# Feature sums by matmul: a moving operand of 1, 2 or 16 columns widened to 128 columns

## The reference

```python
def rmsnorm(x, g):                       # before every mixer and every MLP, and at the end
    var = jnp.mean(x * x, axis=-1, keepdims=True)
    return x * lax.rsqrt(var + EPS) * g

def l2norm(x):                           # over the 128 features of a head
    return x * lax.rsqrt(jnp.sum(x * x, axis=-1, keepdims=True) + 1e-6)

def gated_deltanet(hn, w_in, conv_w, a_log, dt_bias, out_norm_g, w_out):
    proj = hn @ w_in                                   # q, k, v, z, and 2 x 8 logits a token
    qkv = silu(causal_depthwise_conv_2(proj[..., :3 * DN_DIM], conv_w))
    z = proj[..., 3 * DN_DIM:4 * DN_DIM]
    b_raw, a_raw = proj[..., 4 * DN_DIM:...], proj[..., 4 * DN_DIM + DN_HEADS:]
    q, k = l2norm(heads(q)) * DN_HEAD_DIM ** -0.5, l2norm(heads(k))
    beta = sigmoid(b_raw)
    g = -exp(a_log) * softplus(a_raw + dt_bias)
    o = chunk_gated_delta_rule(q, k, v, g, beta)
    o = rmsnorm_2(o, out_norm_g) * silu(z)             # over the 128 features of a head
    return o.reshape(b, t, DN_DIM) @ w_out

# layer 1: attention and a gated recurrence, silu MLP (2816); layer 2: gated_deltanet, squared-relu MLP (4096);
# layer 3: block attention, squared-relu MLP (4096); then the last rmsnorm
```

## Time and profile before

| | |
|---|---|
| time, median of 3 runs | 1207.03 us (1206.67 to 1207.73) |
| profiled execution, its own time | 1205.23 us |
| its span, first to last instruction | 1203.5 us |
| mean TensorE clock granted in it, 1 being full speed | 0.976 |
| PE busy | 1149.0 us, 95% of the span |
| DVE busy | 752.5 us, 63% |
| ACT busy | 564.8 us, 47% |
| POOL busy | 219.4 us, 18% |
| data moved | 187.34 MB, mean 156 GB/s |

### The profile page before, as it was taken

How to read it: one execution, slowest core, us unless ns; L and a number is a source line. 1 busy time by engine, 2 the same in 40 slices (tenths; PEclk the granted TensorE clock), 3 DMA queues, 4 the chain that set the end, 5 groups by cost and what they waited for, 6 DMA issues and landing times.

```text
span 1203.5 us, 21847 instructions
## 1 busy us (share of the span) xinstructions
PE 1149.0 (95%) x8900; PEld 1111.0 (92%) x8900; DVE 752.5 (63%) x913; ACT 564.8 (47%) x721; POOL 219.4 (18%) x226
## 2 busy tenths in 40 slices
PE   4999899999999999999999999999989999999997
PEld 4999889999999999998999998889989999888996
DVE  3755875666566553579968577764466657776433
ACT  4546456535444343456645355543344445554331
POOL 4894001402000000236372020000030002000001
PEclk9999899999999999889989899999989999999999
DMA  9744443654555555335420155555535545555531
GB/s 268 237 150 141 141 141 106 210 175 150 166 184 190 185 175 174 106 122 185 131 89 2 36 161 189 177 186 192 178 106 177 172 132 183 177 187 190 182 139 36
DMA packets 154852, 187.34 MB, mean 156 GB/s; under 512 B 6400, under 2 KB 143776, under 8 KB 154784
## 3 DMA queue, kind: packets, MB, share of 16 engines
q1 hardware_dynamic: 149072, 183.51, 46.9%
q10 hardware_dynamic: 5712, 2.86, 0.9%
HBM read 185.29 MB, written 1.07 MB: 155 GB/s over the span
## 4 chain that ended last, share of the span: by engine, by line
PE 85%; DVE 9%; issue 2%; ACT 2%; DMA 1%; POOL 1%; SPq 0%; DVEq 0%; POOLq 0%; ACTq 0%
PE PS L332 20%; PE PS L334 19%; PE PS L333 19%; PE PS L383 10%; PE PS L385 5%; DVE WL L328 2%; DVE XHL L480 1%; PE PS L392 1%; PE PS L391 1%; PE PS L390 1%; ACT WH L319 1%; PE PS L1793 1%; PE PS L1779 1%; DMA RAW<-in_w_in 1%; PE PS L672 1%
## 5 line engine op out<-in xcount | busy, mean ns | idle before, releaser
L328 DVE TENSOR_TENSOR WL<-RAW,WH 128x2048 fp32r<-128x2048 f32 x173 | 409.0, 2365 | 252.4 <-ACT WH L319 252.4
L319 ACT ACTIVATE WH<-RAW 128x2048 fp32r<-128x2048 f32 x173 | 330.0, 1910 | 248.4 <-PE PS L334 200.8
L332 PE MATMUL PS<-XHL,WH 128*128 128x256 f32 x1184 | 348.9, 295 | 27.6 <-DVE WL L328 17.2
L333 PE MATMUL PS<-XHL,WH 128*128 128x256 f32 x1184 | 342.8, 290 | 0.0
L334 PE MATMUL PS<-XHL,WL 128*128 128x256 f32 x1184 | 342.7, 289 | 0.0
L332 PEld LDWEIGHTS PS<-XHL,WH 128*128 128x128 f32 x1184 | 235.6, 199 | 33.1 <-DVE WL L328 16.9
L333 PEld LDWEIGHTS PS<-XHL,WH 128*128 128x128 f32 x1184 | 235.7, 199 | 0.3
L334 PEld LDWEIGHTS PS<-XHL,WL 128*128 128x128 f32 x1184 | 235.1, 199 | 0.0
L332 PE MATMUL PS<-HH,WH 128*128 (+1 forms) x688 | 195.0, 283 | 4.3 <-DVE SG L1576 2.8
L333 PE MATMUL PS<-HL,WH 128*128 (+1 forms) x688 | 194.7, 283 | 0.0
L334 PE MATMUL PS<-HH,WL 128*128 (+1 forms) x688 | 194.7, 283 | 0.0
(11 more groups left out here) (287 smaller groups left out, 1537.8 us busy)
## 6 DMA issues: line engine op xcount, KB each, us to landing
RAW<-in_mlp_w_up SPq DMA_DIRECT2D x32, 1024.0 KB, 5.4
RAW<-in_mlp_w_down SPq DMA_DIRECT2D x32, 1024.0 KB, 4.9
RAW<-in_w_in SPq DMA_DIRECT2D x28, 1024.0 KB, 5.1
RAW<-in_w_ffn_in_pairs SPq DMA_DIRECT2D x22, 1024.0 KB, 5.1
RAW<-in_dn_w_in SPq DMA_DIRECT2D x16, 1024.0 KB, 5.7
RAW<-in_mb_w_in SPq DMA_DIRECT2D x12, 1024.0 KB, 5.2
RAW<-in_w_ffn_out SPq DMA_DIRECT2D x11, 1024.0 KB, 5.0
RAW<-in_w_attn_out SPq DMA_DIRECT2D x4, 1024.0 KB, 5.2
```

What stands on the lines that cost most here:

```text
L319: act.activation(WH[:, k], RAW[:, k], ACT.Copy).then_inc(hi_done, 1)
L328: dve.tensor_tensor(WL[:, k], RAW[:, k], WH[:, k].bitcast(F32), ALU.subtract).then_inc(lo_done, 1)
L332: pe.matmul(out, wh, xh, start=start, stop=False, skip_group_check=True)
L333: pe.matmul(out, wh, xl, start=False, stop=False, skip_group_check=True)
```

## The change

Every narrow moving operand is made 128 columns wide. The column of ones is taken as the whole 128x128 tile `ONES`, the pair `W2` is repeated 64 times and the 16 logit columns 8 times by a stride of zero. Each result is then 128 columns wide too; of these only the first, the first two or the first 16 are read. The results are laid over each other in PSUM: call n writes columns n to n + 127, so it overwrites all but the first column of call n - 1, and what is read lies where it lay. In the output norm (L1859) the column of head h and token half c moves from 8c + h to 2h + c, so that columns rise in the order in which they are made, and the transposes behind it read them there. The number of instructions and their order on every engine stay as they were, and nothing else is changed.

```diff
@@ norm_sums
                 for c in range(TT):
                     for j in range(KB):
-                        mm = pe.matmul(PS[:, 4, 2 * c:2 * c + 2], XN[:, j, c * P:(c + 1) * P], W2[:, j],
-                                       start=(j == 0), stop=(j == KB - 1))
+                        mm = pe.matmul(PS[:, 4, 2 * c:2 * c + P].rearrange("p (r e) -> p r e", e=2), XN[:, j, c * P:(c + 1) * P],
+                                       W2[:, j, None, :].to_broadcast([P, P // 2, 2]), start=(j == 0), stop=(j == KB - 1))
             else:
                 pe.wait_ge(s_.sq_added, m + 1 - (m > 2))
                 for c in range(TT):
-                    mm = pe.matmul(PS[:, sums_bank(m), c:c + 1], XN[:, 0, c * P:(c + 1) * P], ONES[:, 0:1], start=True, stop=True)
+                    mm = pe.matmul(PS[:, sums_bank(m), c:c + P], XN[:, 0, c * P:(c + 1) * P], ONES[:], start=True, stop=True)
@@ logits, behind dq step 1
                         for k in range(KB):
-                            mm = pe.matmul(PS[:, 3, 256 + 16 * c:272 + 16 * c], H[:, k, c * P:(c + 1) * P], WBA[:, k],
+                            mm = pe.matmul(PS[:, 3, 256 + 16 * c:384 + 16 * c].rearrange("p (r e) -> p r e", e=16),
+                                           H[:, k, c * P:(c + 1) * P], WBA[:, k, None, :].to_broadcast([P, KB, 16]),
                                            start=(k == 0), stop=(k == KB - 1))
@@ l2 norms, behind dz steps 1 and 2
                         sq = (SQK, XN)[u][:, n % 8, (n // 8) * P:(n // 8) * P + P]
-                        mm = pe.matmul(PS[:, 4 + u, n:n + 1], sq, ONES[:, 0:1], start=True, stop=True)
+                        mm = pe.matmul(PS[:, 4 + u, n:n + P], sq, ONES[:], start=True, stop=True)
@@ output norm
                     for c in range(TT):
-                        mm = pe.matmul(PS[:, 4, 8 * c + h:8 * c + h + 1], OSQ[:, h, c * P:(c + 1) * P], ONES[:, 0:1], start=True, stop=True)
+                        mm = pe.matmul(PS[:, 4, 2 * h + c:2 * h + c + P], OSQ[:, h, c * P:(c + 1) * P], ONES[:], start=True, stop=True)
...
-                        at_, n = e * TOK + c * P, 8 * c + 2 * u + e
+                        at_, n = e * TOK + c * P, 4 * u + 2 * e + c
                         mm = pe.transpose(PS[:, RB[u], at_:at_ + P], RNC[:, n:n + 1].to_broadcast([P, P]), IDENT[:])
```

## The result

| | before | after |
|---|---|---|
| median of 6 runs, us | 1206.85 (1206.33 to 1209.23) | 1201.34 (1199.37 to 1201.99) |
| profiled execution, its span, us | 1205.23, 1203.5 | 1201.34, 1199.6 |
| mean granted clock | 0.976 | 0.99 |

The medians differ by 5.5 us. The ratio is 0.995 with a 95% interval of 0.9937 to 0.9963, that is 4.5 to 7.6 us faster. The forecast was 1199.5 in 1196.9 to 1204.3. The part of that range that the forecast held for itself ended at 1200.5; the rival *some falls stay*, with one of its two places, stood at 1201.0.

A forecast was written before the change was run, and what follows sets the result against it. The chain that ended last was 85% PE and 9% DVE, so PE's time counts where PE is awaited. Gains 1.5 + 1.8 + 3.0 + 1.5 = 7.8, less 0.3, leave 7.5 us: 1199.5 us, range 1196.9 to 1204.3.

The forecast's parts named there:

- some falls stay: Rival, chance 0.20: the gaps at L512 and the end of L1859 still bring falls, 1202.5 us; with one of them 1201.0.
- L512, fall at 300: Narrow passes at 298.97 us, after PE idled 1.41 us: the half-clock stretch behind them goes, 1.5 us won (bounds 0 and 1.5).
- L507: Half step behind this burst, 501.11 to 505.55 us: takes 2.9 us instead of 4.44, so 1.5 us won.
- L1706, the burst: Logits burst from 508.85 us: 3.9 us becomes 3.6 at full clock, so 0.3 us won.
- L1706, step 2 behind it: Half-clock work from 512.74 to 518.75 us: 2.6 us to win, priced at nothing because the chain behind `ba_done` hides it.
- second L1720 and last `dz` step: From 601.32 us: burst 4.16 becomes 3.6 us (0.6 won), the step behind it 2.4 won; 3.0 us, all on the path.
- L1859 and `do`: Wide burst to 677.40 us, transposes and two short PE waits: if the clock holds through these, 1.5 us won.
- wider passes: All 180 widened passes: 0.4 us more PE time, partly counted already in other terms, so 0.3 us remains as cost.
- nothing: Rival, chance 0.08: the falls are not due to narrowness, only 0.4 us is added, 1207.4 us.
- The rival of the overlay: Rival, chance 0.04: in calls with ONES, shifted overlapping writes make passes wait for the one before; 9.6 us lost, 1214.8 us.
- absorbed: Rival, chance 0.08: DVE's chain swallows the 1.8 us of `dq`, or POOL the end of `dz`; 2.5 to 3 remain, 1204.3.

The follow-up runs named there:

- the fillers of 128 and 1 columns: The changed kernel plus extra float32 matmuls into an unused bank in three PE gaps, 128 columns wide in one kernel, 1 in the other; 1198.23 and 1198.39 us.

## Why the prediction was right, step by step

| term of the sum | predicted | trace of after | alone |
|---|---|---|---|
| L512, fall at 300 | 1.5 | 1.49 (3.42 us for 4.91) | 1.5 in the trace, 3.1 timed |
| L507 | 1.5 | 1.50 (6.44 for 7.94) | 1.5 in the trace, 2.1 and 1.4 timed |
| L1706, the burst | 0.3 | 0.3 | 0.3 in the trace |
| L1706, step 2 behind it | 0 | 0 | 0 |
| second L1720 and last `dz` step | 3.0 | 3.05 | 3.05 in the trace, 2.9 timed |
| L1859 and `do` | 1.5 | 0.3 (35.78 us for 36.05) | not run |
| wider passes | -0.3 | about 0 | |
| sum | 7.5 | 6.6 | |

The third column sets the trace of after against that of before.

**The clock.** Right at four places of five. That width is the cause, and not chance between executions, is shown by the count over eleven traces (17 of 20 narrow, 0 of 35 wide) and by the fillers of 128 and 1 columns; the rival "nothing" is refuted.

**The cost of the passes.** 32 wide passes take 3.49 us from their first start to the next matmul, 32 narrow ones took 3.50; my 0.4 us for 180 passes was at most that. The table of the Trainium skill that spoke against the change (TensorE: Matmul & The Clock Gate, Back-to-back issue gap) gives more than twice the gap for 128 columns, but for a single matmul on its own. For a stream, as in this kernel, the same section has the spacing set by weight loads and matmuls together, which I had overlooked. This case agrees with the latter: 0.109 us a pass either way, with PEld busy for the whole burst, narrow (3.50 of 3.50 us) and wide (3.50 of 3.50 us, 495.42 to 498.92). The rival of the overlay is refuted in the same rows: L1721, whose calls shift by a column, takes 3.74 us for 32 passes like L1706, whose passes add into the same columns.

**What hides the gain.** The 2.6 us behind L1706 went into PE's waits, as the working had it, but not at AT, the one wait for which it gave a row: that one stayed at 3.18 us, and 3.17 and 3.19 in the kernels with one part. Most of them went into a new wait of 1.68 us for `WL`, at 532.74 with L1706 alone and at 528.30 in after. The rival "absorbed" is refuted: L507 came 2.19 us earlier (495.42 for 497.61) and the transposes behind AT 3.98 (568.28 for 572.26), so the 1.8 us of L507 and L1706 came through.

**The step that failed** is the last: "I take 1.5: 614.80 to 618.20 was nothing but transposes, and the clock stood at 1.00". The clock did hold through the burst and the transposes, but fell at 676.4, just as `do` began, behind 2.02 us in which PE waited for DOL; that wait had even grown, from 1.54 us, since the transposes ahead of it ended earlier. Only 0.3 us was won from the burst to the next layer's matmul, whose rows are, in after and then in before:

```profile
703.59 0.50 PE L383 MATMUL PS<-XHL,WH 128*128 128x512 f32 x1 [0.52 <-DVE XHL L480]
```

```profile
709.95 0.50 PE L383 MATMUL PS<-XHL,WH 128*128 128x512 f32 x1 [0.52 <-DVE XHL L480]
```

Not even this 0.3 is shown to come from the width: over the five traces with a narrow L1859 this stretch took about 36.0 us three times and about 35.2 twice (the fall was 3.4 us long in these two and 6.8 in the others), and with a wide one and no wide fillers 35.8 in all four. So it is the rival *some falls stay*, with one place of its two. That its 1201.0 lies next to the measured 1201.34 is in part luck: the execution in question also lost and won the microseconds of *Not foreseen* below, and the second series of after came out at 1199.96. The row I leaned on, transposes at full clock from 614.80 to 618.20, says nothing on what follows a gap. The Trainium skill would have it (same page, Part 4: PE-mode transpose) that transposes do not count as busy in the same way. No run here settles that, since the wide fillers closed the gap without taking the transposes away; the row at 614.80 speaks against it, as none of the eleven traces has a fall between 612 and 675 us.

**Not foreseen.** The first l2 burst was priced at nothing, since the earlier trace rows has no fall there. Two of the four narrow traces have one, and from the first l2 burst to the transposes behind the second it is 22.7 to 24.4 us in these four and 19.76 in all seven wide ones: the two bursts together are worth 3.0 to 4.6 us, by execution.

In the profiled execution of after, the two MLP stages took 1.5 us longer each, with the clock at 1.00. Groups of their two matmul lines in after, then in before (busy us, mean ns):

```profile
L383 PE MATMUL PS<-XHL,WH 128*128 128x512 f32 x512 | 181.8, 400 | 1.0 <-DVE XHL L480 1.0
L385 PE MATMUL PS<-XHL,WL 128*128 128x256 f32 x512 | 143.8, 281 | 0.0
```

```profile
L383 PE MATMUL PS<-XHL,WH 128*128 128x512 f32 x512 | 178.7, 395 | 1.0 <-DVE XHL L480 1.0
L385 PE MATMUL PS<-XHL,WL 128*128 128x256 f32 x512 | 142.0, 277 | 0.0
```

Other falls moved too: none at 491 (1.3 us won), a shorter one at 894 (0.6 won), a longer one at 567 (1.0 lost), and after was 0.6 us late already when L512 began. 6.6 + 1.3 + 0.6 - 1.0 - 0.6 - 3.0 is 3.9, the difference of the spans (1203.5 and 1199.6). In the second profile of the same kernel the first MLP stage was back at the pace of before and the fall at 894 back at its length (889.0 to 899.3), so these two belong to the execution. For the other two that is not shown: no narrow matmul lies ahead of them, but the fall at 491 is in all five traces without the whole change and in one of the five that have it and no fillers at 491, and the long fall at 567 is in none of the former and in two of the four that have the change and no fillers at 567. The medians, over several executions, put the change at 5.5 and 8.4 us (1208.39 less 1199.96); the sum of the terms, 6.6, lies between.

## What to carry to other kernels

A TensorE that the profile shows as 100% busy may be about to drop to half its clock: look at the granted clock behind every run of matmuls with few moving columns, and widen them to 128 where the weight load already sets their pace, since it cost nothing here. Price a fall only where PE is the one waited for, by the next semaphore that another engine must raise: of the 2.9 us that L1706 gave PE, 0.3 were left behind its waits for `WL` and AT. Where a gap of PE remains ahead of such a place, a few wide dummy matmuls hold the clock, and narrow ones that keep PE just as busy do not.

## What the runs showed of the hardware that was not expected

- The two MLP stages have two paces at clock 1.00, chosen anew by stage and execution: 0.347 or 0.353 us for a pair of passes of 512 and 256 columns (means over 9 us of timeline from 740 and from 1060 us). Before and the kernel with L1706 alone had 0.347 in both stages, after 0.353 in both, the other eight of the eleven one of each. A stage at the slower pace is 1.5 us longer. What sets it stays open.
- Falls are not fixed to a place: the first burst of l2 norms, narrow, had no fall in the earlier trace rows, one of 6.8 us in the kernel with L1706 alone and one of 3.4 us with L507 alone; and the fall at 894 lasted 3.4 us in the first trace of after and 10.2 in the second, with the kernel unchanged. One profile of a kernel therefore shows about which places are at risk, not what each costs on average.
